# Weights laid out in contiguous pieces, one casting queue ordered by first use, bf16 stores spread over three tiles

## The reference, cut to what matters

```python
mod = silu(c) @ w_ada + b_ada                    # (B, 6*1024): shift, scale, gate for two sub-layers
u = rmsnorm(h, norm_mix_w) * (1 + sc_a) + sh_a
q, f_logit, v, g, p = split(u @ w_in)            # w_in 1024 x 2560, five parts of 512
o_rec = hgrn2(q, f_logit, v, g)                  # 4 heads of 128, recurrence over chunks of 32 tokens
o_pool = pool_mixer(p, w_pool, pool_scale)       # trailing means over 2, 4, 8, 16 tokens, minus the token
h = h + gt_a * (concat(o_rec, o_pool) @ w_out)   # w_out 1024 x 1024
u = rmsnorm(h, norm_mlp_w) * (1 + sc_m) + sh_m
h = h + gt_m * (square(relu(u @ w_up)) @ w_down) # w_up 1024 x 4096, w_down 4096 x 1024
return rmsnorm(h, norm_final_w)
```

## Time and profile before

| | |
|---|---|
| median of three runs | 3041.67 us (3030.62 to 3043.46) |
| the profiled execution's own time | 3046.86 us |
| its span on the slowest core (core 0) | 3044.4 us |
| spans of the eight cores | 3014.4 to 3044.4 us |
| busy: PE, DVE, ACT, POOL | 92%, 57%, 47%, 2% |
| DMA moved (a cast counted with its bf16 bytes) | 498.49 MB |
| HBM read, written | 475.03 MB, 57.70 MB |
| first store of tile 0, 1, 2 of the output | 484.3, 661.8, 836.3 us |

### The profile page before, as it was taken

One profiled execution on the slowest core, in us unless ns is written; L12 is line 12 of the kernel. 1 busy time (PEld: TensorE's weight loads), 2 busy tenths in 40 slices (PEclk: granted clock), 3 DMA queues, 4 the chain that ended last, 5 costly groups with the idle time before them and its releaser, 6 DMA issues.

```text
span 3044.4 us, 49254 instructions; the slowest of 8 cores (3014.4 to 3044.4 us)
## 1 busy us (share of the span) xinstructions
PE 2798.4 (92%) x17235; PEld 1440.7 (47%) x17552; DVE 1728.6 (57%) x3278; ACT 1431.2 (47%) x2468; POOL 54.5 (2%) x74
## 2 busy tenths in 40 slices
PE   3157989999999999999999999999999999999998
PEld 1033544545454454545445454545445454544543
DVE  1235644756566475666556565656647566665652
ACT  2125524536364554636364463636455463636431
POOL 2000110000000000000000000000000000000000
PEclk9566999999999999999999999999999999999999
DMA  9972898464454635445453645445364644545343
GB/s 191 170 142 73 159 216 231 139 190 146 149 189 136 204 136 201 139 151 182 145 194 118 221 140 179 160 136 191 132 214 139 205 140 149 185 138 195 118 169 136
DMA packets 177504, 498.49 MB, mean 164 GB/s; under 512 B 15968, under 2 KB 65376, under 8 KB 177264
## 3 DMA queue, kind: packets, MB, share of 16 engines
q1 hardware_dynamic: 126752, 457.88, 45.0%
q0 software_dynamic: 50512, 37.46, 9.8%
HBM read 475.03 MB, written 57.70 MB: 175 GB/s over the span
## 4 chain that ended last, share of the span: by engine, by line
PE 80%; DMA 13%; DVE 2%; issue 2%; another core or an unknown queue 2%; ACT 1%; SPq 0%; DVEq 0%; POOL 0%; ACTq 0%; POOLq 0%
PE pb L480 78%; DMA out<-xh 3%; DMA hidT<-w_ada 3%; PE pb L483 2%; DMA xh<-x 2%; DMA wsl<-wup_s 1%; DMA wsl<-wdn_s 1%; DMA wsl<-w_down 1%; DMA wsl<-w_up 1%; DVE xh L497 1%; DMA wdn_s<-wsl 1%; DVE S L497 0%; DMA wsl<-w_in 0%; DVE pb L490 0%
## 5 line engine op out<-in xcount | busy, mean ns | idle before, releaser
L480 PE MATMUL pb<-u2T,wsl 128*128 128x512 bf16 x3954 | 918.9, 382 | 32.1 <-DMA wsl<-w_up 6.9
L480 PE MATMUL pb<-wsl,hidT 128*128 128x512 bf16 x3965 | 910.5, 379 | 30.0 <-DMA wsl<-wdn_s 13.9
L480 PEld LDWEIGHTS pb<-u2T,wsl 128*128 128x128 bf16 x4096 | 393.0, 98 | 488.6 <-issue 53.2
L480 PEld LDWEIGHTS pb<-wsl,hidT 128*128 128x128 bf16 x4096 | 391.1, 98 | 485.2 <-issue 33.8
L490 DVE TENSOR_SCALAR pb<-pb 128x512 f32<-128x512 f32 x512 | 352.1, 696 | 284.2 <-PE pb L480 279.9
L480 PE MATMUL pb<-wsl,ucT 128*128 128x256 bf16 (+1 forms) x3063 | 478.1, 313 | 7.1 <-DVE S L497 4.0
L486 ACT ACTIVATE hidT<-pb 128x512 bf16<-128x512 f32 x512 | 301.0, 595 | 269.8 <-DVE pb L490 269.0
L494 DVE TENSOR_TENSOR pb<-pb,gbc 128x512 f32<-128x512 f32 x256 | 176.2, 695 | 359.2 <-PE pb L480 358.6
L480 PEld LDWEIGHTS pb<-wsl,ucT 128*128 128x128 bf16 x3072 | 300.1, 99 | 160.2 <-issue 23.0
L480 PE MATMUL pb<-ucT,wsl 128*128 128x512 bf16 x1503 | 339.4, 384 | 5.2 <-DVE ucT L491 2.1
L497 DVE SCALAR_TENSOR_TENSOR S<-S,decs,pb 128x128 f32<-128x128 f32 x1024 | 286.4, 342 | 25.9 <-DVE S L497 11.2
(11 more groups left out here) (82 smaller groups left out, 1874.0 us busy)
## 6 DMA issues: line engine op xcount, KB each, us to landing
wsl<-wup_s SPq DMA_DIRECT2D x240, 512.0 KB, 4.5
wsl<-wdn_s SPq DMA_DIRECT2D x240, 512.0 KB, 3.4
wsl<-win_s SPq DMA_DIRECT2D x150, 512.0 KB, 3.9
xh<-x SPq DMA_DIRECT2D x64, 512.0 KB, 8.8
out<-xh SPq DMA_DIRECT2D x64, 512.0 KB, 7.5
wsl<-wout_s SPq DMA_DIRECT2D x60, 512.0 KB, 4.2
hidT<-w_ada POOLq DMA_DIRECT2D x12, 1024.0 KB, 35.2
wsl<-w_up POOLq DMA_DIRECT2D x16, 512.0 KB, 12.4
```

The source lines that it names most:

```text
L480: return lambda e: e.matmul(out, lhsT=lhsT, rhs=rhs, start=start, stop=stop, **k)
```

## The change

- The host lays every weight out in contiguous pieces: a piece is `[128, 2048]` float32 with 8 KB for each partition, a block of w_ada `[128, 4096]` with 16 KB.
- One list, `casts`, gives the order on POOL for everything up to the end of tile 0 (`at=`, and `line` in the scheduler keeps exactly this order): x of tile 0, the identity, w_ada 0 to 3, the scan mask and other constants, eight w_in pieces, w_ada 4 and 5, the last w_in and the w_out pieces, w_ada 6 to 9, four w_up pieces, x of tile 1, w_ada 10 and 11, the rest.
- x of every tile is now loaded by POOL, not SP. The memsets of S and Sbf move from POOL to DVE. The final norm's weight comes late.
- In the first tile the ring for w_in and w_out may use all eight slots, once.
- With `SPREAD = 3` a w_up or w_down piece is stored in bf16 in tile 0, 1 or 2 (number modulo 3) and is cast from float32 again in every tile up to that one. Tile 0 casts 32 and stores 12 of the 32, tile 1 casts 20 and stores 10, tile 2 casts 10 and stores 10.
- In tile 0 the heads follow their projections at once, the recurrence uses PSUM banks 0, 1, 4 and 5 in pairs, and w_ada 6 to 9 are used block by block. Other tiles keep the order of the code.
- `DMA_RATE` goes from 300e3 to 330e3, which can shift the planned order in all tiles.

```diff
-DMA_RATE = 300e3
+DMA_RATE = 330e3
+SPREAD = 3
...
-        op.prio = (self.base - boost, i)
+        op.prio = (self.base - boost if at is None else at, i)
+        op.line = at is not None
...
+        line = sorted((i for i in range(n) if ops[i].line), key=lambda q: ops[q].prio)
+        head = [0]
+
+        def offer(i):
+            if not ops[i].line or line[head[0]] == i:
+                hpush(future[ops[i].eng], (ready[i], i))
...
-    wada_d = din("w_ada", [D, 6 * D])
+    wada_d = din("w_ada", [12, 128, 4096])
...
-    win_d = din("w_in", [D, 2560])
-    wout_d = din("w_out", [D, D])
-    wup_d = din("w_up", [D, 4 * D])
-    wdn_d = din("w_down", [4 * D, D])
+    win_d = din("w_in", [10, 128, 2048])
+    wout_d = din("w_out", [4, 128, 2048])
+    wup_d = din("w_up", [16, 128, 2048])
+    wdn_d = din("w_down", [16, 128, 2048])
...
+        casts = (xq(0) + [("c", "idn")] + ada(0, 1, 2, 3) + [("c", "scanm"), ("c", "cbt")] + MIX_SEQ[:8] + [("c", "wpool")]
+                 + ada(4, 5) + MIX_SEQ[8:] + ada(6, 7, 8, 9) + MLP_SEQ[:4] + xq(1)
+                 + ada(10, 11) + MLP_SEQ[4:20] + [("c", "wfb")] + MLP_SEQ[20:])
+        CAST_AT = {k: i - 100.0 for i, k in enumerate(casts)}
...
-            P.dma("sp", dm(V(xh, s * D, [[1, D]]), x_d.ap()[r0:r0 + 128, :]), writes=[B_xh[s]], key="x%d" % s,
-                  nbytes=524288)
+            P.dma("pool", dm(V(xh, s * D, [[1, D]]), x_d.ap()[r0:r0 + 128, :]), writes=[B_xh[s]], key="x%d" % s,
+                  nbytes=524288, dur=0.55, at=CAST_AT.get(("x", 4 * t + j)))
...
-            P.dma("pool", dm(V(hidT, so * TT, [[TT, 8], [1, 512]]),
-                             wada_d.ap()[:, hb * 512:(hb + 1) * 512].rearrange("(k p) c -> p k c", p=128)),
-                  writes=B_hid[so:so + 8], key="ada%d" % (hb % 4), nbytes=2097152, dur=0.9)
+            P.dma("pool", dm(V(hidT, so * TT, [[1, 4096]]), wada_d.ap()[hb]),
+                  writes=B_hid[so:so + 8], key="ada%d" % (hb % 4), nbytes=2097152, dur=0.9, at=CAST_AT[("ada", hb)])
...
+        def store_tile(kind, pc):
+            return 0 if kind in ("win", "wout") else min(pc % SPREAD, NT - 1)
...
-                i = self.slots[n % len(self.slots)]
-                if n < len(self.seq):
-                    src, dims = w_src(kind, pc)
-                    P.dma("pool", dm(V(wsl[i], 0, dims), src), writes=[B_w[i]], key="cw%d" % i, nbytes=1048576, dur=0.9)
-                    P.dma("sp", dm(scr[kind].ap()[pc], wsl[i][:]), reads=[B_w[i]], writes=[B_scr[kind][pc]],
-                          key="s_%s%d" % (kind, pc), nbytes=524288)
+                i = self.first[n] if n < len(self.first) else self.slots[n % len(self.slots)]
+                if n < len(self.seq) * (1 + store_tile(kind, pc)):
+                    P.dma("pool", dm(wsl[i][:], SRC[kind].ap()[pc]), writes=[B_w[i]], key="cw%d" % i, nbytes=1048576,
+                          dur=0.55, at=CAST_AT[(kind, pc)] if n < len(self.seq) else None)
+                    if n >= len(self.seq) * store_tile(kind, pc):
+                        P.dma("sp", dm(scr[kind].ap()[pc], wsl[i][:]), reads=[B_w[i]], writes=[B_scr[kind][pc]],
+                              key="s_%s%d" % (kind, pc), nbytes=524288)
...
-        ring_mix = Ring(list(range(NMIX)), MIX_SEQ)
-        ring_mlp = Ring(list(range(NMIX, NMIX + NMLP)), MLP_SEQ)
+        ring_mix = Ring([2, 3, 0, 1], MIX_SEQ, first=[0, 1, 2, 3, 4, 5, 6, 7, 0, 1, 2, 3, 4, 5])
+        ring_mlp = Ring([6, 7, 4, 5], MLP_SEQ)
...
-            head(0)
-            head(1)
+            fq(0)
+            if t == 0:
+                head(0)
+                head(1)
+            fq(1)
...
-                mod_cols(6, 10, 2, 1)
+                for hb in range(6, 10):
+                    mod_cols(hb, hb + 1, 2, 1)
```

More of the change, by code:

```diff
@@ L76, in __init__, with add @@
         self.ops = {e: [] for e in ENGS}
-    def add(self, eng, fns, reads=(), writes=(), dur=0.1, aset=None, dma_key=None, nbytes=0, boost=0.0):
+    def add(self, eng, fns, reads=(), writes=(), dur=0.1, aset=None, dma_key=None, nbytes=0, boost=0.0, at=None):
         op = Op()
@@ L208, in schedule @@
                 if left[j] == 0:
-                    hpush(future[ops[j].eng], (ready[j], j))
+                    offer(j)
+            if o.line:
+                head[0] += 1
+                if head[0] < len(line) and left[line[head[0]]] == 0:
+                    offer(line[head[0]])
             done += 1
@@ L506, in build_nc @@
         MS = 0.0585
+        MIX_SEQ = [("win", i) for i in (2, 0, 3, 1, 6, 7, 4, 5, 8, 9)] + [("wout", i) for i in range(4)]
+        MLP_SEQ = [("wup", i) for i in range(16)] + [("wdn", i) for i in range(16)]
+        ada = lambda *hb: [("ada", i) for i in hb]
+        xq = lambda t: [("x", 4 * t + j) for j in range(4)]
+        casts = (xq(0) + [("c", "idn")] + ada(0, 1, 2, 3) + [("c", "scanm"), ("c", "cbt")] + MIX_SEQ[:8] + [("c", "wpool")]
+                 + ada(4, 5) + MIX_SEQ[8:] + ada(6, 7, 8, 9) + MLP_SEQ[:4] + xq(1)
+                 + ada(10, 11) + MLP_SEQ[4:20] + [("c", "wfb")] + MLP_SEQ[20:])
+        CAST_AT = {k: i - 100.0 for i, k in enumerate(casts)}
         def cload(eng, name, t_, d_, nb):
-            P.dma(eng, dm(t_[:], d_.ap()), writes=C(name), key="c_" + name, nbytes=nb)
+            P.dma(eng, dm(t_[:], d_.ap()), writes=C(name), key="c_" + name, nbytes=nb, at=CAST_AT.get(("c", name)))
         P.base = -30.0
@@ L515, in build_nc @@
             cload("sp", nm_, t_, d_, 16384)
-        P.pool(lambda e: e.memset(epsc[:], EPS), writes=C("eps"))
+        P.pool(lambda e: e.memset(epsc[:], EPS), writes=C("eps"), at=-200.0)
         def x_load(t, j):
@@ L657, in norm_to_T @@
                     P.pe([tr(pbb(bk, (q * 4 + j) * 128, [[1, 128]]), V(xn, j * D + (2 * kp + q) * 128, [[1, 128]]), IDB())
-                          for q in range(2)], reads=[B_xn[j]] + C("cbt"), writes=[B_pb[bk]], dur=2 * MS)
+                          for q in range(2)], reads=[B_xn[j]] + C("idn"), writes=[B_pb[bk]], dur=2 * MS)
                 for q in range(2):
@@ L681, in stage_A @@
             P.label = "A%d" % t
[L682 to L704, removed]
             def head(h):
@@ L738, in head @@
                 P.pe([tr(pbb(6, j * 128, [[1, 128]]), V(koutT, x * TT + j * 128, [[1, 128]]), IDB()) for j in range(4)],
[L739 removed]
+                     reads=[B_koutT[x]] + C("idn"), writes=[B_pb[6]], dur=4 * MS)
                 P.act(actf(V(koutk, h * TT, [[1, TT]]), pbb(6, 0, [[1, 512]]), AF.Copy), reads=[B_pb[6]],
@@ L755, in tokproj, with fq, gate @@
                         P.dve(cp(V(dst, ds * TT, [[1, TT]]), pb[bk][:]), reads=[B_pb[bk]], writes=[Bd[ds]], dur=0.69)
-            head(0)
-            head(1)
+            def fq(hp):
+                wf_ = ring_mix.get("win", 2 + hp)
+                wq_ = ring_mix.get("win", hp)
+                for hh in range(2):
+                    h = 2 * hp + hh
+                    bk = mix_bank()
+                    chunk_mm(wf_, hh * 128, ucT, B_uc, bk)
+                    x = h % 2
+                    P.act(actf(ta[x][:], pb[bk][:], AF.Tanh, scale=0.5), reads=[B_pb[bk]], writes=[B_ta[x]], dur=0.6, aset="A")
+                    P.dve(ts(V(fg, h * TT, [[1, TT]]), ta[x][:], V(omlh, h, [[1, 1]]), V(lbp, h, [[1, 1]]), ALU.mult, ALU.add),
+                          reads=[B_ta[x]] + C("omlh", "lbp"), writes=[B_fg[h]], dur=0.55)
+                for hh in range(2):
+                    h = 2 * hp + hh
+                    bk = mix_bank()
+                    chunk_mm(wq_, hh * 128, ucT, B_uc, bk)
+                    P.act(actf(V(qs, h * TT, [[1, TT]]), pb[bk][:], AF.Silu), reads=[B_pb[bk]], writes=[B_qs[h]], dur=0.6, aset="A")
+            def gate(hp):
+                wg_ = ring_mix.get("win", 6 + hp)
+                for hh in range(2):
+                    h = 2 * hp + hh
+                    bk = mix_bank()
+                    chunk_mm(wg_, hh * 128, ucT, B_uc, bk)
+                    P.act(actf(V(sg, h * TT, [[1, TT]]), pb[bk][:], AF.Silu), reads=[B_pb[bk]], writes=[B_sg[h]], dur=0.6, aset="A")
+            fq(0)
[3 more added lines that the diff above has]
+            fq(1)
+            if t == 0:
+                head(2)
+                head(3)
+            gate(0)
+            gate(1)
+            if t > 0:
+                head(0)
+                head(1)
             tokproj(4, vtok, B_v, "v")
-            head(2)
-            head(3)
+            if t > 0:
+                head(2)
+                head(3)
             tokproj(8, ptok, B_p, "p")
@@ L797, in chain @@
                     v0 = state["sbf"] % NSB
[L798 to L802, removed]
+                    P.dve(lambda e: e.memset(V(S32, s0 * TT, [[1, TT]]), 0.0), writes=[B_S32[s0]])
+                    P.dve(lambda e: e.memset(V(Sbf, v0 * TT, [[1, TT]]), 0.0), writes=[B_Sbf[v0]])
+                wide = 2 if t == 0 else 4
+                bank = lambda jj: (4 - 4 * (jj // 2) if t == 0 else 4 + jj - jj % 2) + jj % 2
```

(11 more changed lines are left out.)

35 lines of the change are left out of this document (14 added, 21 removed).

## The result

The changed kernel takes 0.9886 of the time before (95% interval 0.9856 to 0.9916): faster by 1.1%, some 35 us on 3034.9 us, the median of six runs of the kernel before beside six of the changed one. The profiled execution took 3004.6 us after 3046.9. I had forecast 2960 us with a range of 2915 to 3003; 0.9886 of the 3041.7 that the forecast started from is 3007. The direction was right, the size was not. Ratios here are taken over executions without the disturbance in which the cores of a die run at a lower clock; where too few of these are left for a ratio, a kernel's profiled execution is given.

What follows compares the result with a forecast made beforehand. It took tile 0's start to be bound by weight loading, then the dependent recurrence, and later stretches by PE. Terms -91 + 0 + 10 + 4 - 5 = -82 took 3046.9 to 2965; the runs' median, 5 lower, gave 2960 us, range 2915 to 3003.

Steps and rivals of the forecast that it cites:

- Rate of the casts: Weight casts on POOL's queue: 325 GB/s, with 305 and 337 as near bounds and 238 as the far one.
- Start of UP: Tile 0: UP starts at 180 us instead of 270.6, a gain of 91 us.
- From UP to the first store: Tile 0: stays at 213.7 us, a change of 0 us, from -15 to +15.
- Tiles 1 and 2: Pieces cast again land late: +10 us in tile 1 and +4 in tile 2, from 0 to +30 together.
- the ring's 10.8 us: Tiles 1 and 2: time a ring of four leaves to fill a slot; casts landing at 14.9 us would be late.
- x on POOL, in all tiles: Loads of x moved from SP to POOL, freeing SP's weight loads: -5 us, from -10 to +17.
- later tiles over 176: Sign in the profile: later tiles above 176 us, where 174 was forecast, would mean late x.
- x comes late: Rival: running DVE instructions hold up POOL's descriptors for x, up to 3 us a tile; about 2990 us, chance 0.08.
- The rate rival: Casts stay at 238 GB/s, bound by something other than row length; UP at 224, time 3004 us, chance 0.10.
- the one without any cost: Rival: every kept cost is hidden, rate 337, clock rises early, no piece late; 2918 us, chance 0.17.
- Casts that starve the MLP: Rival: casts land far later, PE stands in each of 30 recast pieces; 3075 us at 28 us landing, chance 0.04.
- No effect: Rival: total traffic sets the end of tile 0, whatever the order; 3042 us, chance 0.03.

Runs made afterwards that it cites:

- e6: Changed kernel with the weights in their old layout (1 KB and 2 KB rows), orders and queues as changed; ratio 1.0006 to the kernel before.
- e5: Changed kernel with SPREAD = 1: all 32 MLP pieces stored in tile 0, none cast again; ratio 0.9922 to the kernel before.
- e11: Changed kernel without the loads of x for tiles 2 to 15, so part of the input is left out; ratio 0.9658 to the kernel before.
- e4: Changed kernel with DMA_RATE back at 300e3 and x of tiles 2 to 15 on SP; ratio 0.9750 to the kernel before.
- e1: Changed kernel with only DMA_RATE back at 300e3, x still on POOL; ratio 0.9779 to the kernel before.
- e3: Kernel before with DMA_RATE 330e3 alone; later tiles 173.0 us against 173.7, profiled execution 3053.7 us.
- e2: Changed kernel with x of tiles 2 to 15 on SP again, DMA_RATE still 330e3; ratio 0.9818 to the kernel before.

## Why the prediction was wrong, by its steps

- **Rate of the casts: right.** I took 325 GB/s; from 50 to 100 us it is 323. The w_ada casts from 15 to 30 us (core 3, after) move 2 x 2.56 MB in 15 us, 341 GB/s, against 305 in the earlier trace rows. Of this gap row length has only the step from 328 (e6) to 341:

```profile
q0 software_dynamic: 345, 2.56, 102.3%
```

- **Start of UP: close, 175.3 for 180** (just under the 176 to 188 given as the sign), with some luck in the steps. The first norm of the recurrence runs at 131.5 (127 forecast), the last norm's product is there at 154.1 (154): the first was 4.5 us late, and the stretch between took 22.6 us, not 27, so the two errors cancel. I had called w_ada 9 no wait; PE stood 2.9 us for it and used it at 149.6. What follows took 21.2 us, not 25.8. The PE timeline of core 3 has w_ada 9, the start of UP and w_ada 10:

```profile
149.56 0.97 PE L493 MATMUL pb<-cact,hidT 128*128 128x4 bf16 x32 [2.92 <-DMA hidT<-w_ada]
...
175.31 6.43 PE L493 MATMUL pb<-u2T,wsl 128*128 128x512 bf16 x16 [1.81 <-DVE u2T L504]
...
195.12 3.28 PE L493 MATMUL pb<-hidT,cact 128*4 128x512 bf16 x8 [2.80 <-DMA hidT<-w_ada]
```

- **From UP to the first store: right**, 210.2 us for 213.7. The forecast wait is in POOL's timeline, 59.8 us for a slot that C frees at 167.2 (166 forecast), but it cost PE little: 2.8 us for w_ada 10, in the lines above, where I had put 9:

```profile
167.16 1.50 POOL L516 DMA_DIRECT2D wsl<-w_up  x2 [59.80 <-PE pb L493]
```

- **Tiles 1 and 2: near**, +7.8 and +10.5 for +10 and +4. The recasts do cost there, 6.0 and 7.7 us by e5, but the landing of casts against the ring's 10.8 us, with which I argued, is not enough as a reason: e11 keeps all recasts and loses nothing. It takes them together with the loads of x; how the two act on each other no run shows. The rest of the loss is the one of every tile, next item.
- **x on POOL, in all tiles: the step that failed.** I wrote -5 us in a range of -10 to +17; it is +44.5. That is 50 us, more than the whole miss of 47 against 3007, and it set off the sign that I had named, later tiles over 176. It has two faults. The small one is a size: I allowed 17 us for x on POOL, and the runs put it at 2.0 us a tile (24 us) in this plan and at 0.5 us (6 us) in the other. The large one is a term put at nothing without a reason: `DMA_RATE`, 4.8 us a tile (58 us) with x on POOL, though I had written that it can shift the order in all tiles, and had read in the chain that x lies on the path where a tile begins. Without both faults, in e4, a later tile is 1.6 us shorter than before. PE's waits for w_up pieces did go away, as forecast: no such row is among those of tiles 3 to 14 on core 3. They were 6 us in 12 tiles.
- **The rival "x comes late"** had the right place and a chance of 0.08, but for a hold on POOL's descriptors. In e1, x is on POOL as well, and the later tiles are within 0.5 us of those with x on SP (e4), while DVE works over 107 us of a tile in the changed kernel. So such a hold is not what made the tiles 3.7 us longer; whether it has a part in the 2.0 us of the other plan no run shows. The Trainium skill describes such a hold in "SBUF — State Buffer" (section SBUF: two separate sides).
- **The rate rival** (238 GB/s) and **the one without any cost** fell: the first by 341 GB/s (and 328 with the short rows of e6), the second by tiles 1 and 2. Casts that starve the MLP were not seen: w_up and w_down casts land in 10.1 and 7.5 us at the median. **No effect** is refuted by the first store.

## What to carry to other kernels

A constant of a planner is an edit to every stage that it orders: before anything else is priced, compare the planned order of one steady tile before and after, multiply what a shift costs by the number of tiles, and ask of each operation that moved forward whether its operand comes sooner as well. A gain of 95 us once was halved by 3.7 us twelve times. And a planner with one rate for all DMAs can't say when a load lands that first waits for a store; giving this one load its own lag brought 4.2 us a tile without moving a byte faster.

## What was not expected of the hardware

The length of a steady tile goes with how long the store and the load at its start take to land, and both are longer where the two cores of a neighbouring pair run close together. In e6 cores 0 and 1 store tile 2 first at 793.8 and 791.1 us, 3 us apart, and then take 178.2 us a tile; cores 6 and 7 are at 793.3 and 774.4, 19 us apart, and take 174.3 and 174.1. The landings on core 0 and then on core 6, from 860 to 2800 us (issues, KB, median us):

```profile
out<-xh SPq DMA_DIRECT2D x44, 512.0 KB, 9.0
xh<-x POOLq DMA_DIRECT2D x44, 512.0 KB, 9.6
```

```profile
out<-xh SPq DMA_DIRECT2D x44, 512.0 KB, 6.3
xh<-x POOLq DMA_DIRECT2D x44, 512.0 KB, 8.4
```

Store and load come one after the other, so 3.9 us more in a row, which is the difference of a tile. The sixteen cores of e6 and the changed kernel fall into two groups. Where the two landings (each a median) add up to 14.4 to 15.1 us, a tile takes 174.1 to 175.2 us and the pair is 9 to 19 us apart at tile 2; where they add up to 17.0 to 18.6, it takes 177.2 to 178.2 and the pair is under 8 us apart. That is no fixed distance, though: in e5 cores 6 and 7 are 9 us apart at tile 2, 3 us at tile 14, and take 177.3 and 178.3. In e3 the pairs that are 11 to 13 us apart take 172.3 to 172.5 us, the ones within 3 us 173.5 to 174.7. The Trainium skill, "HBM Reference" (section Specifications (TRN2)), says that the two cores of a domain share its bandwidth. My guess from both is that the burst at the start of a tile, output, x and w_up pieces, meets the neighbour's. The distance was observed and not set: every core runs one program, so no run here moves one core of a pair alone, and the cause stays argued. It matters for the metric, as the slowest core counts: in the profiled execution of e6 one pair of four sets 3050 us while the other six cores end by 3010.

What also stays open is why 330e3 costs 3.3 us a tile in the changed kernel with x on SP and nothing in the kernel before, with N1 at the same place. PE's waits in tiles 3 to 14 show most of the cost: 32.5 us in all in e2 and 10.5 in e4 on core 3, so 1.8 of the 2.3 us a tile between them there, and 34.1 against 0.7 on core 0, so 2.8 of 3.7. The wait in DOWN is 1.05 us of it and the waits for xn are another 1.1 on core 3. Why the plan makes PE meet them in this kernel and not in the other is not shown.
